# A hybrid stack of three layers: another opening, and side work in fewer steps

## The chip, the cores and the metric

The kernel runs on one core of one Trainium2 chip. The metric is the device time of one execution in microseconds; the lower the better. The kernel before takes 3626.36 us, the median of three runs (3624.73 to 3629.23). A run's time can only be told from another's where they lie apart by more than such spreads.

The engines are called by short names: PE multiplies matrices (PEld loads its weights), DVE and ACT work on vectors element by element, POOL only issues a few transfers here, SP issues the transfers of all weights.

## The reference

Two blocks follow each other on 256 tokens of width 2048, in float32: two hybrid layers (layers 0 and 1 here), then one layer of another kind (layer 2). What matters for this change is the first layer:

```python
mod = jnp.dot(jax.nn.silu(c), w_ada) + b_ada            # c: one vector of 2048, w_ada: 2048 x 6144
shift, scale, gate = jnp.split(mod, 3, axis=-1)
u = rms_norm(x, norm_w) * (1.0 + scale[:, None, :]) + shift[:, None, :]
proj = jnp.dot(u, w_in)                                 # w_in: 2048 x 19064
...
fq, fk  = rms_norm(...)                                 # "fox": 8 heads, full attention with decay
dq, dk  = partial_rope(rms_norm(...), positions)        # "dsa": 8 heads, the keys chosen by an index
iq, ik  = partial_rope(...)                             # 16 index heads of 64: scores, then top 64 of 256
xbc = jax.nn.silu(causal_depthwise_conv(sxbc, conv_w, conv_b))
y = ssd_scan(...)                                       # 4 groups, 2 pieces of 128 tokens
y = y * jax.nn.silu(sz), rms_norm over each group
gates = jax.nn.sigmoid(mg + b_merge)
merged = gates[0] * (y_fox @ w_o_fox) + gates[1] * (y_dsa @ w_o_dsa) + gates[2] * (y_ssd @ w_o_ssd)
x = x + gate[:, None, :] * (merged @ w_out)
```

`u` of the first layer needs `scale` and `shift`, two thirds of a product of one vector with a matrix of 48 MB. They are needed before any projection can start, and their weights are read once only. The same product for layer 1 and the `gate` thirds are worked out later, beside other work.

## The kernel before, in words

**Multiplications.** Every weight matrix is cut into chunks of 1 MB (512 rows by 512 columns, on 128 partitions x 2048). There are 547 of them. To keep float32 precision each factor is split into a high and a low part, and a chunk is multiplied three times (line 1179): high by high, high by low, low by high. A chunk goes through four steps: SP fetches it into a `RAW` buffer (line 1066), ACT copies it rounded into an `HH` buffer (`hi`, line 1434), DVE subtracts and writes the low part into `LL` (`lo`, line 1777; `LL` has the same number as `RAW`), and PE multiplies (`gemm`, in two halves). There are three `HH` buffers and five `RAW`/`LL` buffers; `SP` waits before each fetch until the last reader of its buffer is done, and goes through its fetches in order. What a chunk is multiplied with are `UH`/`UL` (the layer's `u`) or `YH`/`YL`. Chunk numbers below count these multiplications from 0.

**The order.** All engines follow one list of steps written by `work_order` at build time (class `Order`, lines 96 to 345). Between two multiplications stands a `slot`: one step of the lane `evac` (what takes results out of PSUM: `hd` for heads, `conv`, `sz` for the scan's gate, `gate` and `merge`, ...) and one of the lane `side` (everything else: the angles `rope`, the small projections `misc`, index scores `ix`, the selection `ix_top`/`ix_sel`, attention `att`, the scan `ssd`). A lane is a queue of generators; a `yield` ends a step. `yield MID` says that the next part is to be placed between the two halves of the next multiplication (`middle`). Where a multiplication needs the result of a lane's job, `until` takes slots without multiplications until that job is done. `ada_maybe` puts in, at a rate `every`, chunks of `w_ada` of layer 1 and of the `gate` thirds, which DVE multiplies with the vector (`ada`, line 1794, four instructions each) and PE folds (`fold`, line 1207).

**The opening** (`open`, lines 311 to 341) works out `scale` and `shift` of layer 0 in four groups of 4 x 128 columns. In a group there are eight column blocks of 1 MB, four of `scale` and four of `shift`. Five of the eight are summed by DVE from a transposed copy of the weights (`dot_dve`, line 1770: one instruction over 2048 elements with a sum), three by PE (`dot_pe`, line 1196: 16 products with one column each, in two passes, so 32 rows). Then `am` (lines 1864 to 1876) adds the biases, and `u` (lines 1906 to 1929) modulates 512 columns of x on DVE, with ACT's rounded copy (line 1477) and DVE's difference (line 1928) behind it. As soon as `u` has a group, three chunks of projections (two of `iq`, one of `dk`) are multiplied beside the sums of the next group. In the opening there are three more `RAW` buffers, eight in all, used in turn for everything that is fetched. Before the first group x is normalized on ACT (line 1447), turned by PE (line 1217) and copied (line 1438). The angle work `rope`, for tokens and for channels in two parts each (lines 1812 to 1850, on `WW`, tiles `W`), is spread over slots of the first three groups.

**Buffers at the end of the opening.** Fetches 42 and 43 (the last two chunks of the third projection step) go into buffers 0 and 1 again; buffer 0 was last given to chunk 9's weights. Fetch 42 so waits until multiplication 9 is done.

## Time and profile before

| | |
|---|---|
| median of three runs | 3626.36 us |
| the profiled execution | 3630.86 us, its span 3629.1 us |
| PE busy | 3487.7 us (96%), 18836 instructions |
| PE's weight loads | 2994.2 us (83%) |
| DVE busy | 2268.1 us (62%) |
| ACT busy | 1689.1 us (47%) |
| granted TensorE clock, mean | 0.977 |
| DMA | 706.72 MB, mean 195 GB/s |

The profiled execution is one execution of the program; the rows further down are of it. The span runs from the first to the last instruction, and 1.8 us lie around it. Busy time of PE counts pipelined matmuls, so that a matmul of 0.39 us stands beside the next one that starts earlier. In a row of the trace the form `out<-in` names the tiles without their numbers, and what stands in brackets at the end is how long the engine had been idle before, and who released it. A stretch (`A:B`) gives for each engine the busy time and the number of instructions in it, then the clock that was granted to PE (1.00 is 2.4 GHz, 0.50 would be 1.2 GHz throughout), the busy share of the 16 DMA engines and the rate of the transfers.

### The profile page before, as it was taken

Reading aid. Unit: us, or ns where it says so; the run is one execution under the profiler, and the core shown is the slowest. Engines: PE = TensorE matmul, PEld = TensorE weight load, DVE = VectorE, ACT = ScalarE, POOL = GpSimd, SP = SyncE. Lnnn points to the kernel's source line nnn. Section 1 sums busy time; section 2 is a strip of 40 time slices with the busy share of each in tenths; the row PEclk is TensorE's granted clock in tenths of the full one; section 3 lists DMA queues with packets and bytes.
Section 4 is the critical chain, followed back from the end, with each engine's and each line's share of the span. In section 5 each row is a group of like instructions: output and inputs, shape, how many; then the busy total and the mean of one; then the engine's idle time right before and its main releaser. Section 6 shows DMA issues by size and latency. Waiting matters only on the chain. (4 is left out here: it accounts for less than half of the span.)

```text
span 3629.1 us, 45020 instructions
## 1 busy us (share of the span) xinstructions
PE 3487.7 (96%) x18836; PEld 2994.2 (83%) x18836; DVE 2268.1 (62%) x2673; ACT 1689.1 (47%) x2077; POOL 31.1 (1%) x61
## 2 busy tenths in 40 slices
PE   8889999997999999999999999999999999999998
PEld 7779878877887887789888788888888789988887
DVE  5568766765667656677656566765566667554544
ACT  3254654353343334545653553333445775443433
POOL 0000000000000000000000000000000000000000
PEclk8899999998999999999999999999999999999999
DMA  8654445445767655444444357765555443455554
GB/s 346 264 187 149 165 174 209 175 150 203 263 254 272 239 186 197 164 162 151 163 146 145 128 204 258 266 253 195 184 188 185 171 163 142 151 219 186 194 184 154
DMA packets 99531, 706.72 MB, mean 195 GB/s; under 512 B 11696, under 2 KB 11712, under 8 KB 15616
## 3 DMA queue, kind: packets, MB, share of 16 engines
q1 hardware_dynamic: 93888, 675.38, 50.7%
q0 software_dynamic: 4864, 24.95, 2.0%
q8 instruction: 149, 2.44, 0.3%
q10 hardware_dynamic: 576, 3.50, 0.3%
q14 instruction: 54, 0.44, 0.0%
HBM read 697.49 MB, written 6.29 MB: 194 GB/s over the span
## 5 line engine op out<-in xcount | busy, mean ns | idle before, releaser
L1434 ACT ACTIVATE HH<-RAW 128x2048 fp32r<-128x2048 f32 x546 | 1044.8, 1914 | 1204.2 <-PE G L1179 853.8
L1777 DVE TENSOR_TENSOR LL<-RAW,HH 128x2048 fp32r<-128x2048 f32 x546 | 1247.7, 2287 | 349.3 <-ACT HH L1434 347.7
L1179 PE MATMUL G<-HH,UH 128*128 128x512 f32 x2528 | 1019.9, 403 | 38.0 <-DVE LL L1777 35.0
L1179 PE MATMUL G<-LL,UH 128*128 128x512 f32 x2528 | 998.1, 395 | 0.0
L1179 PE MATMUL G<-HH,UL 128*128 128x512 f32 x2528 | 997.9, 395 | 0.0
L1179 PE MATMUL G<-UH,HH 128*128 128x256 f32 x2080 | 607.6, 292 | 17.6 <-DVE XS L2029 9.0
L1179 PEld LDWEIGHTS G<-HH,UH 128*128 128x128 f32 x2528 | 483.2, 191 | 156.3 <-DVE LL L1777 45.3
L1179 PE MATMUL G<-UH,LL 128*128 128x256 f32 x2080 | 592.8, 285 | 0.0
L1179 PE MATMUL G<-UL,HH 128*128 128x256 f32 x2080 | 592.6, 285 | 0.0
L1179 PEld LDWEIGHTS G<-LL,UH 128*128 128x128 f32 x2528 | 482.4, 191 | 103.8
L1179 PEld LDWEIGHTS G<-HH,UL 128*128 128x128 f32 x2528 | 483.4, 191 | 100.9 <-issue 3.6
L1179 PEld LDWEIGHTS G<-UH,HH 128*128 128x128 f32 x2080 | 403.2, 194 | 27.1 <-DVE LL L1777 22.2
L1179 PEld LDWEIGHTS G<-UL,HH 128*128 128x128 f32 x2080 | 403.2, 194 | 2.3 <-issue 1.5
L1179 PEld LDWEIGHTS G<-UH,LL 128*128 128x128 f32 x2080 | 402.6, 194 | 0.0
L1179 PE MATMUL G<-HH,YH 128*128 128x512 f32 x768 | 306.6, 399 | 3.2 <-DVE LL L1777 3.2
L1179 PE MATMUL G<-LL,YH 128*128 128x512 f32 x768 | 304.6, 397 | 0.0
L1179 PE MATMUL G<-HH,YL 128*128 128x512 f32 x768 | 304.3, 396 | 0.0
L1794 DVE SCALAR_TENSOR_TENSOR ACC<-RAW,CT,ACC 128x512 f32<-128x512 f32 x240 | 180.1, 751 | 9.1 <-DMA RAW<-in_w_ada_packed_dram 2.2
L1179 PEld LDWEIGHTS G<-HH,YH 128*128 128x128 f32 x768 | 144.8, 188 | 39.9 <-DVE LL L1777 5.7
L1179 PEld LDWEIGHTS G<-HH,YL 128*128 128x128 f32 x768 | 144.8, 189 | 34.8 <-issue 0.2
L1179 PEld LDWEIGHTS G<-LL,YH 128*128 128x128 f32 x768 | 144.6, 188 | 34.9
L1993 DVE SCALAR_TENSOR_TENSOR S<-G,PAR,S 128x253 f32<-128x253 f32 x144 | 69.2, 480 | 52.2 <-ACT S L1535 48.7
(353 smaller groups left out, 2522.0 us busy)
## 6 DMA issues: line engine op xcount, KB each, us to landing
RAW<-in_w_in_packed_dram SPq DMA_DIRECT2D x402, 1024.0 KB, 4.8
RAW<-in_w_ada_packed_dram SPq DMA_DIRECT2D x76, 1024.0 KB, 4.9
RAW<-in_w_out_packed_dram SPq DMA_DIRECT2D x48, 1024.0 KB, 4.8
RAW<-in_w_o_ssd_packed_dram SPq DMA_DIRECT2D x32, 1024.0 KB, 4.8
RAW<-w_ada_turned_packed_dram SPq DMA_DIRECT2D x20, 1024.0 KB, 12.4
RAW<-in_w_o_fox_packed_dram SPq DMA_DIRECT2D x16, 1024.0 KB, 6.1
RAW<-in_w_o_dsa_packed_dram SPq DMA_DIRECT2D x16, 1024.0 KB, 5.8
RAW<-in_w_proj_a_packed_dram SPq DMA_DIRECT2D x16, 1024.0 KB, 4.8
```

The lines of the kernel that those rows point to most:

```text
L1179: mm = pe.matmul(to, lt, rh, start=first, stop=end, skip_group_check=True)
L1434: a.activation(HH[g % NH][:, :n], RAW[buf(ch["f"])][:, :n], ACT.Copy).then_inc(*hi_done.up(g))
L1777: v.tensor_tensor(LL[buf(f)][:, :n], RAW[buf(f)][:, :n], HH[g % NH][:, :n].bitcast(F32), ALU.subtract).then_inc(*lo_done.up(g))
L1794: v.scalar_tensor_tensor(ACC[:, :], src, CT1[:, kk:kk + 1], ACC[:, :], ALU.mult, ALU.add).then_inc(*ada_acc.up(i, k))
L1993: v.scalar_tensor_tensor(to, of, weight(j), to, ALU.mult, ALU.add).then_inc(*done.up(*key, n))
```

## The change

The change has six parts.

1. *Rings of buffers.* In the opening the column sums get buffers 0 to 3 in turn (`"dots"`), the projection chunks 5, 6, 7 and 4 (`"first"`). Behind the opening, as before, all go through 0 to 4.
2. *Column sums.* In the first group three sums stay on PE, in the others one; DVE takes the rest, 26 in all for 20 before, PE 6 for 12. `am` adds the parts accordingly.
3. *Modulation on ACT.* In layer 0 `u` is worked out on ACT (`Identity` with scale and bias) in place of DVE.
4. *Angle work and x.* The slots of the opening are now in the first group, behind its sums 2 to 7, so that `scaled` and all four `rope` parts stand there; `x_norm` and `x_in` come three sums later.
5. *Side work in fewer steps.* Two `ix_top` to a step; the scan's last step of the first piece (`ssd_y`, c = 0) and the next piece's first step in one slot (`MID`); `misc_sp` 2 and `misc_cs` in one.
6. *Rate of `ada`.* Two slots in five for one in two, from the end of the opening to the convolution.

```diff
--- before.py
+++ after.py
@@ -29,6 +29,12 @@
 NR, NX, NH = 5, 3, 3
+
+
+RINGS = {"dots": (0, 1, 2, 3), "first": (5, 6, 7, 4), "all": tuple(range(NR))}
+
+
+ON_PE = (3, 1, 1, 1)
 HEADS = {"iq": (None, "idx", 4), "dk": ("dsa", "rot", 2), "dq": ("dsa", "rot", 4), "fq": ("fox", None, 4),
@@ -107,7 +113,7 @@
         self.packed = {}
-        self.opening, self.next_buf, self.buf_user = True, 0, {}
+        self.turn_of, self.buf_user = {}, {}
         self.fetches = []
@@ -158,23 +164,24 @@
-    def fetch(self, src, reader):
+    def fetch(self, src, reader, ring="all"):
         name = src[0]
         self.packed[name] = self.packed.get(name, 0) + 1
         f = len(self.fetches)
-        buf = self.next_buf % (NR + NX if self.opening else NR)
-        self.next_buf += 1
+        bufs = RINGS[ring]
+        buf = bufs[self.turn_of.get(ring, 0) % len(bufs)]
+        self.turn_of[ring] = self.turn_of.get(ring, 0) + 1
         self.fetches.append({"src": src, "at": (name, self.packed[name] - 1), "reader": reader, "buf": buf,
                              "before": self.buf_user.get(buf)})
         self.buf_user[buf] = f
         return f
-    def bring(self, ch):
+    def bring(self, ch, ring="all"):
         ch["g"] = len(self.chunks)
         self.chunks.append(ch)
-        ch["f"] = self.fetch(ch["src"], ("gemm_done", ch["g"]))
+        ch["f"] = self.fetch(ch["src"], ("gemm_done", ch["g"]), ring)
         self.put("hi", ch["g"])
@@ -305,7 +312,7 @@
         token = ("dot_" + engine, kind, ct)
-        self.dots[token[1:]] = self.fetch(src, token)
+        self.dots[token[1:]] = self.fetch(src, token, "dots")
         self.put(*token)
@@ -313,29 +320,30 @@
             old = [b["chunks"][gi - 1] if gi else None for b in blocks]
-            dots = [("shift", 1, "pe"), ("scale", 0, "dve"), ("scale", 1, "dve"), ("shift", 2, "pe"), ("scale", 2, "dve"),
-                    ("scale", 3, "dve"), ("shift", 3, "pe"), ("shift", 0, "dve")]
+            on_pe = [("shift", m, "pe") for m in range(4 - ON_PE[gi], 4)]
+            dots = [("scale", m, "dve") for m in range(4)] + [("shift", m, "dve") for m in range(4 - ON_PE[gi])]
+            for i, part in zip((0, 3, 6) if gi == 0 else (2,), on_pe):
+                dots.insert(i, part)
             for i, (kind, m, engine) in enumerate(dots):
                 if i == 7:
                     new = blocks[0]["chunks"][gi]
-                    self.bring(new)
+                    self.bring(new, "first")
                 self.dot(kind, 4 * gi + m, engine)
                 if i in (2, 5) and gi:
                     ch = old[1 + i // 5]
-                    self.bring(ch)
+                    self.bring(ch, "first")
                     self.put("lo", ch["g"])
                 if i in (0, 3) and gi:
                     self.gemm(old[i // 3])
-                    self.slot()
                 if not gi:
                     between(i)
+                    if i > 1:
+                        self.slot()
             enter(gi)
             if gi < 3:
                 self.put("lo", new["g"])
             if gi:
                 self.gemm(old[2])
-                self.slot()
-        self.opening, self.next_buf = False, 0
         self.pend.append(blocks[0]["chunks"][3])
@@ -353,10 +361,10 @@
     def first_x(i):
-        if i == 1:
+        if i == 4:
             put("x_norm", 0)
             put("x_norm", 1)
-        if i == 3:
+        if i == 6:
             for c in range(KT // 2):
@@ -575,7 +583,8 @@
                 put("ix_top", l, qt, i)
-                yield
+                if i % 2:
+                    yield
             put("ix_sel", l, qt)
@@ -595,7 +604,7 @@
                 side_ended("ssd_yd", l, g, c)
-                yield
+                yield None if c else MID
     def misc(l):
@@ -615,7 +624,6 @@
         put("misc_sp", l, 2)
-        yield
         put("misc_cs", l)
@@ -676,7 +684,7 @@
             o.ada["list"] += [(1, b, k) for b in range(8) for k in range(4)]
-            o.ada["every"] = (1, 2)
+            o.ada["every"] = (2, 5)
             misc_b = o.block([one], misc(l), ("U", 0), u_ready, KT)
@@ -1472,6 +1480,17 @@
         def u(l, gi):
+            if l == 0:
+                a.wait_ge(*am.at(0, gi))
+                a.wait_ge(*x_put.at(KT // 2 - 1))
+                for pi in (2 * gi, 2 * gi + 1):
+                    if pi >= 2:
+                        a.wait_ge(*u_lo.at(0, pi - 2))
+                    for j in range(2):
+                        ct = 2 * pi + j
+                        i = a.activation(SS[pi % 2][:, j * S:(j + 1) * S], xsT[:, ct, :], ACT.Identity,
+                                         bias=SH[:, ct:ct + 1], scale=AM[:, ct:ct + 1])
+                    i.then_inc(*u_full.up(0, pi))
             for pi in (2 * gi, 2 * gi + 1):
@@ -1813,6 +1832,7 @@
             if part == 0:
+                v.wait_ge(*ld_cst.at())
                 v.wait_ge(*ld_pos[r].at())
@@ -1863,17 +1883,17 @@
         def am_first(gi):
             c = 4 * gi
+            e = c + 4 - ON_PE[gi]
             pe_part = (BD, BE)[gi % 2]
             v.wait_ge(*ld_mod.at())
             v.wait_ge(*ld_par[0].at())
-            v.wait_ge(*dot_dve.at("shift", c))
+            v.wait_ge(*dot_dve.at("shift", e - 1))
             v.tensor_tensor(AM[:, c:c + 4], DOT[:, 16 + c:20 + c], MOD[:, 16 + c:20 + c], ALU.add).then_inc(*own.up())
-            v.tensor_tensor(SH[:, c:c + 1], DOT[:, c:c + 1], MOD[:, c:c + 1], ALU.add).then_inc(*own.up())
+            v.tensor_tensor(SH[:, c:e], DOT[:, c:e], MOD[:, c:e], ALU.add).then_inc(*own.up())
+            v.wait_ge(*dot_pe.at("shift", c + 3))
+            v.tensor_tensor(SH[:, e:c + 4], pe_part[:, e - c:4], MOD[:, e:c + 4], ALU.add).then_inc(*own.up())
             v.wait_ge(*own.last())
-            v.scalar_tensor_tensor(AM[:, c:c + 4], AM[:, c:c + 4], 1.0, PA[:, c:c + 4], ALU.add, ALU.mult).then_inc(*own.up())
-            v.wait_ge(*dot_pe.at("shift", c + 3))
-            v.wait_ge(*own.last())
-            v.tensor_tensor(SH[:, c + 1:c + 4], pe_part[:, 1:4], MOD[:, c + 1:c + 4], ALU.add).then_inc(*am.up(0, gi))
+            v.scalar_tensor_tensor(AM[:, c:c + 4], AM[:, c:c + 4], 1.0, PA[:, c:c + 4], ALU.add, ALU.mult).then_inc(*am.up(0, gi))
         def am_v(l, gi):
@@ -1905,20 +1925,17 @@
         def u(l, gi):
             for step in range(3):
-                if step < 2:
+                if step < 2 and l:
                     pi = 2 * gi + step
-                    if l:
-                        v.wait_ge(*xn_turned.at(l, pi))
-                    elif pi == 0:
-                        v.wait_ge(*x_put.at(KT // 2 - 1))
+                    v.wait_ge(*xn_turned.at(l, pi))
                     if pi >= 2:
                         v.wait_ge(*u_lo.at(l, pi - 2))
                     else:
                         v.wait_ge(*evac_before("u", l, gi))
-                    v.wait_ge(*am.at(l, 0 if l else gi))
+                    v.wait_ge(*am.at(l, 0))
                     for j in range(2):
                         ct = 2 * pi + j
-                        src = TURN[gi % 2][step][:, j * S:(j + 1) * S] if l else xsT[:, ct, :]
+                        src = TURN[gi % 2][step][:, j * S:(j + 1) * S]
                         i = v.tensor_scalar(SS[step][:, j * S:(j + 1) * S], src, AM[:, ct:ct + 1], SH[:, ct:ct + 1], ALU.mult,
```

What this does to the order is shown at three places, each before and then after. Line numbers of the new kernel are some lines higher: L1789 is the column sum (L1770 before), L1796 the split `lo` (L1777 before).

The first place is DVE in the first group, from the first column sum to the first split of a chunk. `RAW,DOT<-RAW,CB` are column sums, `WW` the angles, `RST` the norm of x, `AM` and `SH` the entry. Before:

```order
L1770 SCALAR_TENSOR_TENSOR RAW,DOT<-RAW,CB 128x2048
L1854 RECIPROCAL RST<-RST 128x1 x2
L1770 SCALAR_TENSOR_TENSOR RAW,DOT<-RAW,CB 128x2048 x4
L1870 TENSOR_TENSOR AM<-DOT,MOD 128x4
L1871 TENSOR_TENSOR SH<-DOT,MOD 128x1
L1873 SCALAR_TENSOR_TENSOR AM<-AM,PAR 128x4
L1876 TENSOR_TENSOR SH<-BD,MOD 128x3
L1922 TENSOR_SCALAR S<-XS,AM,SH 128x256 x4
L1928 TENSOR_TENSOR UL<-S,UH 128x512 x2
L1777 TENSOR_TENSOR LL<-RAW,HH 128x2048
```

and now, with the angle instructions that follow each other cut to the first ones (`...`):

```order
L1789 SCALAR_TENSOR_TENSOR RAW,DOT<-RAW,CB 128x2048 x2
L1829 TENSOR_SCALAR PAR<-PAR 128x1
L1848 CAST WW<-WW 128x2
...
L1789 SCALAR_TENSOR_TENSOR RAW,DOT<-RAW,CB 128x2048
L1874 RECIPROCAL RST<-RST 128x1 x2
L1854 TENSOR_SCALAR WW<-WW 128x96
...
L1789 SCALAR_TENSOR_TENSOR RAW,DOT<-RAW,CB 128x2048
L1843 CAST WW<-WW 128x256
...
L1789 SCALAR_TENSOR_TENSOR RAW,DOT<-RAW,CB 128x2048
L1891 TENSOR_TENSOR AM<-DOT,MOD 128x4
...
L1945 TENSOR_TENSOR UL<-S,UH 128x512 x2
L1796 TENSOR_TENSOR LL<-RAW,HH 128x2048
```

All angle work moved in front of the first `AM`, the norm's reciprocals moved behind the third sum, and the four modulations (`S<-XS,AM,SH`) are gone from DVE.

The second place is DVE at the scan's gate in layer 0: `SM`, `XS` and `S` rows belong to `sz`, `MOD` to a fold, `ACC` to `ada`, `LL` to the chunks. PE's transpose for `XS<-BE,PAR` stands between the row above it and that row. Before, at the last group of the gate:

```order
L1777 TENSOR_TENSOR LL<-RAW,HH 128x2048
L2022 RECIPROCAL SM<-SM 128x1
L2024 TENSOR_SCALAR XS<-XS,SM 128x512
L2029 TENSOR_TENSOR XS<-BE,PAR 128x512
L2014 SCALAR_TENSOR_TENSOR S<-S,G 128x512
L2017 SCALAR_TENSOR_TENSOR XS<-S,XS 128x512
L2022 RECIPROCAL SM<-SM 128x1
L2024 TENSOR_SCALAR XS<-XS,SM 128x512
L2029 TENSOR_TENSOR XS<-BE,PAR 128x512
L1806 TENSOR_TENSOR MOD<-BE,MOD 128x4
```

and now at the same last group:

```order
L1796 TENSOR_TENSOR LL<-RAW,HH 128x2048
L2046 TENSOR_TENSOR XS<-BE,PAR 128x512
L2031 SCALAR_TENSOR_TENSOR S<-S,G 128x512
L2034 SCALAR_TENSOR_TENSOR XS<-S,XS 128x512
L1796 TENSOR_TENSOR LL<-RAW,HH 128x2048
L2039 RECIPROCAL SM<-SM 128x1
L2041 TENSOR_SCALAR XS<-XS,SM 128x512
L1796 TENSOR_TENSOR LL<-RAW,HH 128x2048
L2046 TENSOR_TENSOR XS<-BE,PAR 128x512
L1825 TENSOR_TENSOR MOD<-BE,MOD 128x4
```

and at the second group, where a fold now stands:

```order
L1796 TENSOR_TENSOR LL<-RAW,HH 128x2048
L2046 TENSOR_TENSOR XS<-BE,PAR 128x512
L2031 SCALAR_TENSOR_TENSOR S<-S,G 128x512
L2034 SCALAR_TENSOR_TENSOR XS<-S,XS 128x512
L2039 RECIPROCAL SM<-SM 128x1
L2041 TENSOR_SCALAR XS<-XS,SM 128x512
L2046 TENSOR_TENSOR XS<-BE,PAR 128x512
L1825 TENSOR_TENSOR MOD<-BE,MOD 128x4
L1810 TENSOR_SCALAR ACC<-RAW,CT 128x512
L1813 SCALAR_TENSOR_TENSOR ACC<-RAW,CT,ACC 128x512 x3
```

Before, the last two steps of the gate and the fold stood between two multiplications, with no `LL` row between them. Now an `LL` row stands between each pair there, and the pile is at the second group instead.

The third place is DVE at the small projections of layer 0. `WW<-WW 40x256` are `misc_sp` 2, `FF`, `T` and `CS` are `misc_cs`, `RR` and `S` a head (`hd`), and PE's `misc_turn` waits for the end of `misc_cs`. Before:

```order
L2126 TENSOR_TENSOR WW<-WW 40x256
L2128 SCALAR_TENSOR_TENSOR WW<-WW 40x256
L1777 TENSOR_TENSOR LL<-RAW,HH 128x2048
L1939 RECIPROCAL SM<-SM 128x4
L1946 SCALAR_TENSOR_TENSOR S<-G,SM,ROWS 128x128 x4
L1962 TENSOR_TENSOR RR<-S,RT 128x128
L1963 TENSOR_TENSOR RR<-S,RT 128x4x16
L1964 TENSOR_TENSOR RR<-S,RT 128x4x16
L1966 TENSOR_TENSOR S<-RR 128x4x32
L2142 SCALAR_TENSOR_TENSOR FF<-CST,WW 8x256
L2145 TENSOR_SCALAR FF<-FF 8x256
```

and now:

```order
L1983 TENSOR_TENSOR S<-RR 128x4x32
L2134 TENSOR_SCALAR WW<-WW 40x256
L2136 SCALAR_TENSOR_TENSOR WW<-WW 40x256
L2137 SCALAR_TENSOR_TENSOR WW<-WW 40x256
L2139 RECIPROCAL WW<-WW 40x256
L2141 TENSOR_TENSOR WW<-WW 40x256
L2143 TENSOR_TENSOR WW<-WW 40x256
L2145 SCALAR_TENSOR_TENSOR WW<-WW 40x256
L2159 SCALAR_TENSOR_TENSOR FF<-CST,WW 8x256
L2162 TENSOR_SCALAR FF<-FF 8x256
```

Before, a chunk's split and a head stood between the two parts. Now they are one piece behind the head.

## Rows read from the trace of the kernel before

**Rows 1.** Stretches: PE, PEld, DVE, ACT, POOL busy; clock, DMA share, GB/s.

```profile
38.90:73.60 34.70, 34.16 (x172) 30.00 (x172) 23.43 (x34) 9.65 (x8) 0.00 (x0) 0.74 0.85 346
73.60:106.50 32.90, 32.90 (x169) 28.39 (x168) 28.80 (x49) 8.02 (x8) 0.00 (x0) 0.81 0.84 335
106.50:141.70 35.20, 35.20 (x175) 30.27 (x175) 21.39 (x23) 7.01 (x5) 0.00 (x0) 0.80 0.71 291
...
20.00:40.00 20.00, 15.76 (x89) 14.41 (x89) 9.67 (x13) 13.61 (x16) 0.00 (x0) 1.00 1.02 423
343.00:375.00 32.00, 30.17 (x246) 29.21 (x245) 28.33 (x55) 14.07 (x20) 0.00 (x0) 1.00 0.42 151
800.00:900.00 100.00, 75.22 (x491) 69.83 (x490) 56.01 (x60) 39.70 (x35) 2.13 (x4) 0.87 0.51 186
```

**Rows 2.** DVE in order of time: start, duration, line, operation, tiles; the opening.

```profile
38.94 0.16 DVE L1870 TENSOR_TENSOR AM<-DOT,MOD 128x4 f32<-128x4 f32 x1
...
41.36 1.38 DVE L1922 TENSOR_SCALAR S<-XS,AM,SH 128x256 f32<-128x256 f32 x4
...
73.64 0.16 DVE L1870 TENSOR_TENSOR AM<-DOT,MOD 128x4 f32<-128x4 f32 x1
...
141.70 0.17 DVE L1870 TENSOR_TENSOR AM<-DOT,MOD 128x4 f32<-128x4 f32 x1
```

**Rows 3.** PE in order of time, opening and early layer 0.

```profile
54.90 3.63 PE L1196 MATMUL BE<-CT,RAW 128*128 128x1 f32 x32
...
59.28 0.63 PE L1179 MATMUL G<-HH,UH 128*128 128x512 f32 x1
...
62.58 0.39 PE L1179 MATMUL G<-LL,UH 128*128 128x512 f32 x1
...
62.81 0.39 PE L1179 MATMUL G<-HH,UH 128*128 128x512 f32 x1
...
163.90 0.79 PE L1179 MATMUL G<-HH,UH 128*128 128x512 f32 x1 [9.02 <-DVE LL L1777]
...
208.12 0.80 PE L1179 MATMUL G<-HH,UH 128*128 128x512 f32 x1 [4.40 <-DVE LL L1777]
...
258.50 0.44 PE L1268 MATMUL BA<-CST,T 128*128 128x128 f32 x2 [2.55 <-ACT T L1653]
```

**Rows 4.** SP in order of time, behind the opening.

```profile
154.91 1.87 SPq L1066 DMA_DIRECT2D RAW<-in_w_in_packed_dram  x4
```

**Rows 5.** The W tiles alone, 0 to 200 us, columns as in rows 1.

```profile
0.00:200.00 200.00, 0.00 (x0) 0.00 (x0) 10.19 (x36) 1.40 (x4) 1.06 (x2) 0.85 0.74 294
```

**Rows 6.** Line 1770, the column sums on DVE: shortest/median/longest ns, starts.

```profile
L1770 DVE SCALAR_TENSOR_TENSOR RAW<-RAW,CB x20: 2280/2288/2293, 16.4 to 139.3; 128x2048 f32<-128x2048 f32 x20
```

**Rows 7.** ACT in order of time: entry, and a convolution step.

```profile
42.13 1.28 ACT L1477 ACTIVATE UH<-S 128x512 fp32r<-128x512 f32 x2 [2.14 <-DVE S L1922]
...
275.51 0.56 ACT L1535 ACTIVATE S<-G,PAR 128x256 f32<-128x256 f32 x1 [4.63 <-PE G L1179]
```

**Rows 8.** DVE in order of time: small projections and selection, layer 0.

```profile
242.50 0.29 DVE L2117 TENSOR_SCALAR WW<-WW 40x256 f32<-40x256 f32 x1
...
246.33 0.42 DVE L2128 SCALAR_TENSOR_TENSOR WW<-WW 40x256 f32<-40x256 f32 x1
...
362.31 0.42 DVE L2242 MAX8 SM<-WW 128x8 f32<-128x256 f32 x1
...
364.27 2.29 DVE L1777 TENSOR_TENSOR LL<-RAW,HH 128x2048 fp32r<-128x2048 f32 x1
```

**Rows 9.** PE's waits, 800 to 900 us: total us, times, longest.

```profile
PE BE L1286 <- DVE XS L2024: 12.2, 3, 7.3
PE G L1179 <- DVE XS L2029: 5.3, 1, 5.3
...
PE BE L1207 <- DVE XS L2029: 0.9, 1, 0.9
```

**Rows 10.** The page, costliest groups: the `ada` products on DVE.

```profile
L1794 DVE SCALAR_TENSOR_TENSOR ACC<-RAW,CT,ACC 128x512 f32<-128x512 f32 x240 | 180.1, 751 | 9.1 <-DMA RAW<-in_w_ada_packed_dram 2.2
```

## The prediction, made before the changed kernel was run

> **What bounds the kernel now.** I read the page first, then the stretches, then the opening on each engine in order of time, then PE's waits. On the page PE is busy for 3487.7 of 3629.1 us, so only what PE waits for, what it does needlessly, and its clock are worth anything: 141 us of idle time. The stretches show two places where most of that lies: the first 200 us, and 800 to 900 us, where PE is busy for 75 us at a granted clock of 0.87 [rows 1]. The rest of the change must be read against a PE that is full.
>
> In the opening the reader should see the cadence of the four groups. Each ends with the first instruction of `am` on DVE: four such rows, the first at 38.9, the second at 73.6, the last at 141.7 us [rows 2], on average 34.3 us apart; three of the stretches are cut there. In these three stretches PE is busy all the time (34.2 of 34.7, then 32.9 and 35.2 in full) at a granted clock of 0.74 to 0.81, DVE for 21 to 29 us, DMA at a share of 0.71 to 0.85 [rows 1]. PE sets the cadence. A group on PE is three column sums of 3.63 us [rows 3] and three chunk multiplications, which so take (34.3 - 10.9) / 3 = 7.8 us each. They would be shorter at full clock: behind a column sum the matmuls take 0.63 us (at 59.28), and some 3 us later 0.39 (at 62.58) [rows 3], the 1.2 and the 2.4 GHz level. At the higher one they start 0.23 us apart (62.58 and 62.81), 24 of them in 5.6 us.
>
> At the end of the opening PE waits 9.0 us at 163.90 [rows 3]: four weight fetches in a row could start only at 154.91 [rows 4], because the next buffer was still read by the multiplication before.
>
> **The opening after the change.** Loads of a group, each against the cadence of 34.3:
> - PE: one column sum in place of three, 3 x 7.8 + 3.6 = 27.0 us at the clock of before, less if the stretches at 1.2 GHz go with the sums.
> - DVE: 73.6 us busy in the three groups [rows 1], of which some 9.8 us are angle work (10.2 us on the W tiles up to 200 us [rows 5], 36 instructions, all in this opening) that now stands in the first group. That leaves 21.3 a group; minus 1.4 for the modulation that ACT takes over, plus two more sums of 2.2 (2.29 us each, 20 of them now [rows 6], overlapping by 0.08) = 24.3, plus a wait for ACT of about 2.3 inside each entry = 26.6 us.
> - ACT: the modulation. On DVE four instructions took 1.38 us [rows 2]. ACT with scale and bias per partition took 0.56 us for one of this size out of PSUM [rows 7]; out of SBUF no row shows it. Bounds: 1.4 us for four (as DVE) to 2.3 (4 x 0.56); I take 2.1, nearest the only ACT row. ACT is idle enough to hide it, but the entry is a chain, DVE's split waits behind it: +0.7 us a group.
> The Trainium skill (ScalarE: Activation LUTs, Rules for kernel authors) advises VectorE and not ScalarE for multiply and add, and its section What ACT_TABLE_LOAD costs gives 186 ns + 0.833 ns an element + about 93 ns for each per-partition operand. An estimate from that is 0.585 us each, about 2.1 us for four; the trace agrees with its 0.56. By the rule alone the move would cost 0.7 us in each of four entries.
> - DMA: 11 transfers of 1 MB. From 20 to 40 us the DMA share is 1.02 at 423 GB/s [rows 1], 2.48 us a transfer: 27.3 us.
> So three resources meet at 27, and that is the floor. I take 29.5 for the second and third interval: the modulation ring has four buffers, SP issues in order, and one buffer in each turn is held by PE's sum, which stands behind a multiplication that itself waits for the entry. Two or three fetches stand behind it, and DMA idles for 2 to 3 us.
>
> The first group gets later. All the angle work comes into it: 11.3 us of DVE time with its gaps. It fits partly into the time that DVE now waits there for transfers, but the norm's reciprocals, the transposes and ACT's copies of x queue behind the sines. Walking down the new order with the durations above: four sums, four angle parts, `am` at about 45 us instead of 38.9 (41 with PE's part, behind which the modulation starts at 41.36 [rows 2]), and the first multiplication at about 54 us. The ring then refills only from there, so the first interval is 33 us. `am` of the last group: 45 + 33 + 2 x 29.5 = 137 us against 141.7.
>
> The end of the opening gains more. The buffers of the last fetches are freed by sums that are done long before, so the 9.0 us wait goes. From `am` to the second multiplication behind it: 0.5 + 2.1 + 1.3 (ACT's two copies [rows 7]) + 0.7 + 2.2 for the split (2.29 us at 364.27 [rows 8]) + 7.3 for one multiplication = 14 us, before 163.9 - 141.7 = 22.2. It starts at 151 instead of 163.9: **-13 us**. Bounds: -27 (`am` first at 41, as now, then 27.3 three times: 123 + 14 = 137) and -2 (45 + 3 x 34.3 + 14 = 162).
>
> **The side work after the change.** It changes nothing in what is computed, only how many steps share one multiplication.
> - *Gating in layer 0* (`sz`). PE now waits 12.2 us in three waits of its transposes for VectorE, 5.3 for a gate chunk and 0.9 for the fold [rows 9]: 18.4 us. The last six `sz` steps and a fold stand between two multiplications. Now fox attention ends four chunks sooner, and each of the last steps has a multiplication beside it. What is late next: a pile of the same kind behind chunk 87, with half a multiplication (2.8 us) to cover it: 7.3 - 2.8 + 0.9 = 5.4 us, and one transpose of 4.1. Loss 9.5 (with the longest wait of 7.3 [rows 9] and a guess of 4.1, a third of the 12.2) for 18.4, and about 4 of the 10 us that the clock of 0.87 takes from the 75 busy ones [rows 1]: **-13**, bounds -18 and 0 (a wait that proves to be the weights' DMA stays).
> - *`misc_sp` 2 and `misc_cs` in one step.* In layer 0 they now run between a `hd` and PE's `misc_turn`. The part moved in is 242.50 to 246.75, 4.25 us [rows 8]; now PE waits 2.55 us at that place [rows 3]. With one half multiplication less it becomes some 7 to 8: **+5**, bounds 0 and +6. In layer 1 the step stands alone, nothing.
> - *`ix_top` two to a slot.* From 343 to 375 us DVE is busy 28.3 of 32 us [rows 1], so it already is nearly the bound in a slot of 6.5 us; one pair of 8-wide maxima at 256 takes 362.31 to 364.27, 1.96 us [rows 8]. Four slots get 1.4 to 2 us more than they have room for; lookahead hides one or two us of about 7: **+5**, bounds 0 and +8.
> - *`gate` 0, an `ada` chunk and `gate` 1 piled up* behind chunks 106, 118 and 130, where PE now waits for nothing: 0.7 + 3.0 + 2.2 + 0.7 us of DVE against one multiplication of 5.6: **+3**, bounds 0 and +5.
> - *Fewer `ada` chunks early* (2 in 5 for 1 in 2): one chunk of four, some 3 us (4 x 0.75 [rows 10]), leaves the path in front of the 4.4 us wait at 208.12 [rows 3]: **-3**, bounds -4 and 0.
> Sum: -13 - 13 + 5 + 5 + 3 - 3 = **-16 us**. Against the profiled execution's 3630.9 us (span 3629.1, 1.8 us around it) that is 3615; the median of the three runs, 3626.4, is 4.5 us lower, so I forecast **3610 us**.
>
> **Rivals.**
> - *B, the loads decide* (cadence 27.3, the first group hides its angle work). For it: DVE waits for transfers in the first group, and PE's clock may rise with six sums fewer. Against: SP's queue is in order, and DVE, DMA and PE would have to fit with no slack at all. -27 in place of -13: 3596.
> - *C, the ring of four keeps the old cadence.* Before, up to eight transfers were under way; now four for sums. If each PE sum blocks the queue as long as PE takes for a multiplication at the low clock, the intervals stay near 34: -2 in place of -13, side work as above: 3621; with the gating worth nothing too, 3634. Taken together about 3626.
> - *D, slower: VectorE becomes the bound where side work was packed.* One mechanism: from chunk 30 to 57 each slot in layer 0 gets the convolution and a bigger step (two maxima; then attention up to chunk 47; then two steps of the scan with a fold, against a multiplication of some 6 us). It decides if DVE needs over 7 us a slot in more than ten slots: 10 to 15 slots x 2 us = +25 in place of +5, opening as forecast: 3630 to 3640, say 3635. For it: 28.3 of 32 us busy [rows 1]. Against: the attention slots cost PE an extra us too, and the same work is missing later.
>
> **Chances.** Forecast 0.48, its own range 3600 to 3620; B 0.20; C 0.17; D 0.15. What a measurement here can tell from no change is about 0.2%, 7 us. Faster takes B and nearly all of the forecast, 0.65; same takes C and the forecast's upper edge, 0.20; slower takes D, 0.15. The range runs from B's 3592 to 3633, where half of D is left out.
>
> **What the profile will show.** `am` at 45, 78, 107, 137 us; if it is 41, 68, 96, 123 then B, if the intervals are 34 then C. DMA share near 0.9 in these intervals and SP waiting for PE's sum. Column sums on PE: 6 behind 3.6 us each, granted clock above 0.85 from 50 to 140. No 9 us wait in front of the second multiplication behind the last `am`. Between the last attention step and the fg chunks in layer 0 PE waits of 9 us in place of 18, the largest at a transpose. A wait of 7 to 8 us at `misc_turn` in layer 0. DVE over 95% busy for four slots around 320 to 345 us. The forecast is wrong if the start of the second multiplication behind the opening moves by under 5 us, or if PE's idle time between 250 and 600 us grows by over 15.

## The result and the profile after

The changed kernel takes 3646.23 us (median of nine runs, 3640.01 to 3648.63) for 3629.23 before on the same chips: 1.0044 of it, 95% interval 1.0033 to 1.0055. It is 0.44% slower (17 us), where 16 us less were forecast. Its profiled span is 3640.9 us, 11.8 more than before.

The first view is the table of stretches. Its first three lines are the groups of the opening and answer to the first three of [rows 1], the last to the last there:

```profile
44.37:78.58 34.21, 24.80 (x108) 20.00 (x106) 24.03 (x23) 11.73 (x13) 0.00 (x0) 0.80 0.73 286
78.58:108.81 30.23, 23.51 (x104) 19.59 (x104) 24.09 (x24) 8.85 (x9) 0.00 (x0) 0.83 0.91 365
108.81:139.52 30.71, 24.36 (x106) 19.57 (x104) 24.20 (x23) 8.87 (x9) 0.00 (x0) 0.83 0.95 383
...
800.00:900.00 100.00, 86.15 (x538) 78.74 (x537) 67.81 (x70) 39.84 (x34) 1.60 (x3) 0.91 0.56 208
```

PE is no longer full in the opening (25 of 34 us), and in the second and third stretch the transfers nearly are (0.91 and 0.95). From 800 to 900 us PE is busy for 86 us, 75 before. DVE in order of time answers to [rows 2]; the two entries between these start at 78.58 and 108.81:

```profile
44.37 0.16 DVE L1891 TENSOR_TENSOR AM<-DOT,MOD 128x4 f32<-128x4 f32 x1
...
139.52 0.16 DVE L1891 TENSOR_TENSOR AM<-DOT,MOD 128x4 f32<-128x4 f32 x1
```

and ACT in order of time shows the modulation where [rows 7] had only its stand-in:

```profile
47.37 2.06 ACT L1491 ACTIVATE S<-XS,SH,AM 128x256 f32<-128x256 f32 x4
```

PE in order of time answers to [rows 3]: the first multiplication behind the last `am`, the first row of the second (the 25th from there; no wait stands in front of it), and `misc_turn`:

```profile
146.24 0.79 PE L1187 MATMUL G<-HH,UH 128*128 128x512 f32 x1 [6.46 <-DVE LL L1796]
...
153.92 0.39 PE L1187 MATMUL G<-HH,UH 128*128 128x512 f32 x1
...
239.90 0.69 PE L1276 MATMUL BA<-CST,T 128*128 128x128 f32 x2 [8.01 <-ACT T L1672]
```

PE's waits from 750 to 1160 us answer to [rows 9] and reach further, since a wait that was not there before stands on top (two small ones, 3.1 us together, are left out):

```profile
PE G L1187 <- ACT WW L1597: 10.7, 4, 2.7
PE BE L1294 <- DVE XS L2041: 8.8, 4, 4.7
PE G L1187 <- DVE LL L1796: 7.0, 5, 2.5
PE BE L1215 <- DVE YL L2086: 5.1, 1, 5.1
...
```

**A ledger by chunk.** Both kernels have the same chunks, so the start of ACT's copy `HH` of chunk g, minus the same start before, says how far ahead (-) a kernel is. Worked out from the timelines, one profiled execution of each kernel, in us (`new opening alone` is `o_only` below, `with the new rate` `o_rate`, `with MID only` `o_mid`):

| chunk | new opening alone | with the new rate | with MID only | changed kernel |
|---|---|---|---|---|
| 10 | -16.1 | -17.1 | -14.3 | -16.5 |
| 20 | -9.7 | -21.3 | -10.4 | -21.2 |
| 40 | -9.7 | -12.2 | -8.8 | -4.0 |
| 60 | -9.7 | -22.5 | -9.5 | 0.5 |
| 85 | -8.9 | -22.8 | 7.0 | 14.9 |
| 98 | -2.9 | -36.6 | 0.4 | -18.9 |
| 150 | -1.7 | -13.3 | -0.7 | 3.7 |
| 250 | -3.3 | -13.8 | 0.7 | -0.3 |
| 260 | -3.3 | -13.8 | 12.4 | 13.3 |
| 300 | -3.2 | -13.8 | 11.6 | 12.6 |
| end | -4.2 | -12.3 | 10.8 | 11.8 |

The last column tells where the time went: 21 us won by chunk 20 (half of it, the rate's, is gone again by chunk 30, in `o_rate` too), lost again by chunk 60, won once more at the gating (chunk 98), lost in the merge branches (98 to 150) and in layer 1 (250 to 260).

Such a column can be read to some 5 us only. `a_phase1` and `a_fix` below have the same order of work as the changed kernel up to the merge branches. Yet at chunk 85 they stand at 20.8 and 18.8 us, where the changed kernel stands at 14.9. In chunks 80 to 85 the same 224 instructions took PE 46.5 us in the changed kernel and 49.7 in each of the other two, at a granted clock of 1.00 and 0.93, with no wait.

### The profile page after: what moved, and what is told of

It reads as the page before. It is cut to its first block and busy times, and to the rows that moved or that the text cites. A ratio compares the mean times of both kernels' runs of the same rounds, so it can differ in the third digit from the quotient of the medians.

```text
span 3640.9 us, 44638 instructions
## 1 busy us (share of the span) xinstructions
PE 3465.1 (95%) x18644; PEld 2968.7 (82%) x18644; DVE 2276.1 (63%) x2669; ACT 1703.2 (47%) x2099; POOL 31.1 (1%) x61
## 5 line engine op out<-in xcount | busy, mean ns | idle before, releaser
L1796 DVE TENSOR_TENSOR LL<-RAW,HH 128x2048 fp32r<-128x2048 f32 x546 | 1248.2, 2287 | 365.5 <-ACT HH L1442 364.2
L1187 PE MATMUL G<-UH,HH 128*128 128x256 f32 x2080 | 607.6, 292 | 18.9 <-DVE LL L1796 12.5
L1187 PEld LDWEIGHTS G<-UH,HH 128*128 128x128 f32 x2080 | 403.2, 194 | 27.7 <-DVE LL L1796 22.8
```

Source lines behind the costliest of these rows:

```text
L1187: mm = pe.matmul(to, lt, rh, start=first, stop=end, skip_group_check=True)
L1796: v.tensor_tensor(LL[buf(f)][:, :n], RAW[buf(f)][:, :n], HH[g % NH][:, :n].bitcast(F32), ALU.subtract).then_inc(*lo_done.up(g))
```

## Experiments

Times are medians; the kernel before took 3629.7, 3629.8, 3631.3 and 3631.4 us in the four groups of runs. "The kernel of 3591 us" in the expectations is `best` below.

**One part alone.** `o_only` is the changed kernel with four lines put back:

```diff
-                if i % 2:
-                    yield
+                yield                               # ix_top
-                yield None if c else MID
+                yield                               # scan
+        yield                                       # between misc_sp 2 and misc_cs
-            o.ada["every"] = (2, 5)
+            o.ada["every"] = (1, 2)
```

> The new opening (rings, column sums, modulation on ACT, angle work) with all side work as before. Theory 1 (the opening gave what its stretch shows, and side work took it back): the copy of chunk 20 stands 18 to 21 us earlier than before, and the gap stays to the end; about 3611 us, 0.5% faster than before. Theory 2 (time gained in the opening is given back by whatever stands behind it, as the clock or the weights' transfers): the gap shrinks behind chunk 30; 3622 to 3632 us.

Measured 3626.36 us, ratio 0.9991 (0.9982 to 1.0000): a miss for theory 1, whose 18 to 21 us by chunk 20 were the opening's and the rate's together. The time is that of theory 2, but the gap does not shrink behind chunk 30: the opening's own 9.7 us stand in the ledger (8.9 at chunk 85); then, up to chunk 90, 6 go, with the same order of work as before and no new wait. A stretch of chunks 86 to 88 shows most of it, first in the kernel before:

```profile
726.38:747.14 20.76, 20.76 (x104) 15.63 (x104) 13.62 (x26) 9.70 (x24) 0.00 (x0) 1.00 0.23 87
```

and with the new opening alone:

```profile
717.43:742.95 25.52, 25.52 (x105) 19.37 (x104) 14.29 (x26) 9.70 (x25) 0.00 (x0) 0.80 0.19 72
```

The work is the same and the granted clock differs. What lowered it is open. These are two single executions, and the clock can differ so between executions of one order, as above; but the medians agree that of the 9.7 us some 3 are left.

`o_rate` keeps the `(2, 5)`, `o_mid` the `MID`:

> The new opening and, of the side work's changes, only the rate of two slots in five. Theory 1 (the rate alone sets against which steps of the gate and of the scan's gating a fold falls): the pile of six sz steps and a fold behind chunk 94 is gone, the piles behind chunks 106, 118, 130 and 142 are there, each with a PE wait of 2.7 us for ACT; -16 there, +18 here, -2 early: within 5 us of the kernel with the new opening alone, 3611 us. Theory 2 (what moved the piles is that fox attention ended four chunks earlier, as the prediction said): both piles as before, since attention is not shortened here; 3608 us from the early gain alone.

> The new opening and, of the side work's changes, only the scan's joined steps (MID). Theory 1 (the joined step costs in both layers): layer 1 is 12 to 16 us longer between chunks 250 and 275, with PE waiting for DVE in its decay products, and layer 0 by some 5; 3625 to 3632 us. Theory 2 (the loss of layer 1 belongs to attention that begins earlier behind shorter selection): layer 1 within 3 us of before from chunk 245 to 300; 3611 us.

`o_rate`: 3612.29 us, 0.9957 (0.9945 to 0.9970). Attention is not shortened in it, yet the pile at chunk 94 goes and the four piles at the gates come: theory 1. Of the 12.2 us in three waits of [rows 9] this is left in it from 750 to 1160 us:

```profile
PE BE L1294 <- DVE XS L2041: 3.1, 3, 1.3
```

Its gain is 14 us over `o_only`, more than either expected. A third pile, behind chunk 54, goes too (PE waits 1.0 us there for 4.0): 14 us between chunks 54 and 60, of which half are lost again by chunk 70. `o_mid`: 3638.30 us, 1.0025 (1.0015 to 1.0036), 12 us slower than `o_only`, most of it between chunks 250 and 260: theory 1 (its 3625 to 3632 stood on an `o_only` of 3611).

**The four waits of 2.67 us.** In the merge branches one slot of the changed kernel holds `gate` 0, an `ada` chunk, `gate` 1 and a `merge`. On ACT, in order of time:

```profile
907.36 1.91 ACT L1442 ACTIVATE HH<-RAW 128x2048 fp32r<-128x2048 f32 x1 [3.17 <-PE G L1187]
909.18 0.61 ACT L1597 ACTIVATE WW<-WW 128x512 f32<-128x512 f32 x1
```

and on PE:

```profile
909.93 0.47 PE L1187 MATMUL G<-HH,UH 128*128 128x512 f32 x1 [2.67 <-ACT WW L1597]
```

The gate's `tanh` stands in ACT's queue behind a chunk's copy; the copy waits for the end of PE's multiplication, and PE's next one waits for the `tanh`: 1.91 + 0.61 us and the signals. DVE's work is not in it: the product of the merge waits for the same `tanh` (2.70 us). `a_phase1` moves the `ada` counter on by one slot ahead of the branches, so that folds fall elsewhere:

```diff
         o.ada["every"] = (1, 3)
+        o.ada["count"] += 1
```

> The changed kernel, and the ada counter is moved on by one slot ahead of the merge branches, so that no fold falls against a gate. Theory 1 (the four piles cost 4 x 5 us): none of the waits of 2.7 us for ACT is left between chunks 100 and 152, 18 us less than the changed kernel, 3628 us. Theory 2 (the multiplications there are slower for another cause, as the clock): 3 us or less; 3643 us.

3632.98 us, ratio 1.0008 (0.9999 to 1.0017), 13 less than the changed kernel: nearer to theory 1. The four waits are gone, and at chunk 150 it is 19 us ahead of the changed kernel; but the line runs in layer 1 too, and puts two folds against gates there: PE waits 5.3 us in two waits for the same row. `a_fix` and `best` (on `o_rate`) have `+= 1 if l == 0 else -1`:

> The changed kernel with the counter one slot further in layer 0's merge branches and one back in layer 1's, so that no fold falls against a gate in either layer. Theory 1 (six waits of 2.67 us told the two kernels apart; none is left): 3628 us, 18 less than the changed kernel. What it then stands above 3591 us (37 us) is the price of the three joined steps together. Theory 2: the shift is worth no more than in the kernel with the shift in both layers: 3633 us.

> The new opening with the rate of two in five, all other side work as before, and the ada counter one slot further in layer 0's merge branches (and one back in layer 1's, where the shift alone had put two folds against gates). Theory 1 (each fold against a gate costs about 5 us): the four PE waits of 2.67 us for ACT are gone and none comes in layer 1; 18 us less than with the rate alone, about 3594 us. Theory 2 (the shift only moves the loss to another place, as it did in layer 1): 3608 to 3615 us.

3628.82 us, 0.9993 (0.9984 to 1.0003), and 3591.22 us, 0.9892 (0.9879 to 0.9906). The piles cost 17 us in the changed kernel and 21 in `o_rate`: theory 1 both times. In `best`, which runs up to 45 us ahead there, PE's waits from 750 to 1120 us are these:

```profile
PE G L1188 <- DVE LL L1797: 6.3, 5, 2.4
PE BE L1295 <- DVE XS L2042: 3.0, 3, 1.3
PE G L1188 <- DVE XS L2047: 2.2, 1, 2.2
```

The waits for ACT and the one of 5.1 us for `YL` are gone with the shift, in `a_fix` as well. The 8.8 us for `XS` are still there in `a_fix`; they belong to the joined steps.

**The joined steps, one by one**, added to `best` (the lines of the change), and the scan's taken from `a_fix`:

> The kernel of 3591 us (new opening, rate of two in five, no fold against a gate), with two ix_top to a step added. Theory 1 (the prediction's: DVE has 1.4 to 2 us too much in four slots): 5 us slower, 3596 us, layer 0 alone. Theory 2 (all but the first slot is hidden): within 2 us.

> The kernel of 3591 us, with misc_sp 2 and misc_cs in one step added. Theory 1: PE's wait at misc_turn in layer 0 grows from 2.5 to 8 us and nothing gives it back, 5.5 us slower, with a dip of the granted clock behind it perhaps 7: 3597 us. Theory 2 (the step saved is won later): within 2 us.

> The changed kernel without folds against gates (3629 us), and with the scan's joined steps undone. Theory 1 (the joined steps cost 10 us in layer 0, for the gating's pile behind chunk 87 then has attention in it, and 14 in layer 1): 3605 us, and this is the 3591 us kernel plus 10 and 4 for the two other joins. Theory 2 (the joins of selection and small projections cost more together than alone): 3612 us or more.

`b_ix` 3601.13 (0.9920, 0.9908 to 0.9933), `b_misc` 3595.43 (0.9906, 0.9893 to 0.9920), `a_nomid` 3598.08 us (0.9911, 0.9896 to 0.9926). So `ix_top` costs 10 alone (twice theory 1 of `b_ix`), the small projections 4 (near theory 1 of `b_misc`, and within the spread of the runs), both together 7 (3598.1 - 3591.2), and `MID` 31 us (3628.8 - 3598.1): `a_nomid` is 7 us below its theory 1, and `MID` costs more than there and than alone. That the two others don't add up is not shown: at chunk 250 `b_ix` stands 7.0 us behind `best`, `b_misc` 2.0 and `a_nomid` 8.9. From chunk 280 to 290 `a_nomid` then wins 4.7 of them, with the same 416 instructions on PE: 85.5 us at a granted clock of 1.00, where the kernel before and `best` have 90.2 us at 0.94.

The stretch from chunk 250 to 260, without `MID` (`a_nomid`):

```profile
1738.00:1807.00 69.00, 68.25 (x341) 56.23 (x340) 39.17 (x40) 41.06 (x84) 0.00 (x0) 1.00 0.42 150
```

and with it (`a_fix`):

```profile
1751.50:1833.50 82.00, 77.95 (x369) 63.41 (x368) 43.27 (x47) 48.89 (x94) 0.00 (x0) 0.94 0.36 128
```

No engine but PE is near its bound. `a_fix` does more in its stretch (369 instructions on PE for 341), and waits more. What is late is one chain: with `ssd` and the first decay step under one multiplication, PE reaches the scan's product before DVE has its operand. PE in order of time, in `a_fix`:

```profile
1809.08 3.68 PE L1385 MATMUL BD<-XD,WW 128*128 128x64 f32 x16 [2.38 <-DVE WW L2295]
```

and the same product, the third of eight in layer 1, in `a_nomid`, where none of them waits:

```profile
1796.57 1.89 PE L1385 MATMUL BD<-XD,WW 128*128 128x64 f32 x16
```

From chunk 250 to 290 PE waits 6.7 us in `a_fix` and 1.1 in `a_nomid`. The clock comes on top: PE's busy time, times one minus the granted clock, summed over stretches of ten chunks, is 11 us for 0. Of these 11 only 6 are the joined step's, for the kernel before and `best` lose 5 there as well (chunks 280 to 290 above). A ledger of the two kernels gives 13 us for layer 0 (up to chunk 250) and 17 for layer 1, of which 4.7 are that clock. Between `o_mid` and `o_only`, where `MID` stands alone, it gives 4 us for layer 0 and 11 for layer 1. Layer 1 thus agrees (12.7 and 11); why layer 0 costs 13 in company and 4 alone, no run here takes apart.

**The opening's parts**, each undone on `best`: modulation on DVE by the old `u` (`b_udve`), and

```diff
-ON_PE = (3, 1, 1, 1)                               # b_pe3
+ON_PE = (3, 3, 3, 3)
-            for i, part in zip((0, 3, 6) if gi == 0 else (2,), on_pe):
+            for i, part in zip((0, 3, 6), on_pe):
-RINGS = {"dots": (0, 1, 2, 3), "first": (5, 6, 7, 4), "all": tuple(range(NR))}     # b_ring8
+RINGS = {"open": tuple(range(NR + NX)), "all": tuple(range(NR))}
+        ring = ring if ring == "all" else "open"
-                    if i > 1:                      # b_rope; slots behind the multiplications
-                        self.slot()                # of groups 2 to 4 again, x_norm at i == 1,
                                                    # x_in at i == 3
```

`n_rate` is the kernel before with only the rate and the counter's shift.

> As the kernel of that last row, with the modulation of the first layer back on DVE. Theory 1 (four entries, each with four operations of 0.52 us on ACT for 0.35 on DVE): 3 us faster than with ACT, since the entry is a chain. Theory 2 (DVE's relief is worth more): 3 to 6 us slower, since DVE's sums stand behind it.

> As that kernel, with three column sums of every group on PE. Theory 1 (PE with three sums set the cadence of 34 us): am of the last group moves from 139.5 to 146 us or later, 7 to 12 us slower. Theory 2 (the rings set it): within 3 us.

> As that kernel, with all fetches of the opening through one ring of eight buffers. Theory 1 (what the rings gave is the wait of 9.0 us at the second multiplication behind the opening, and what they cost is about 3 us of DMA time in each group): the cadence falls from 30.5 to 28.5 us and the wait of 9 is back; 3 us slower in all. Theory 2 (the ring of four costs nothing in the groups): 9 us slower.

> The kernel of 3591 us with the angle work back in the second and third group and x normalized earlier in the first. Theory 1 (the angle work delays the first am by 5 us and the later groups are bound by the loads, so they hide it): am first at 39 us, the later ones 3 to 5 us earlier, 3587 us. Theory 2 (DVE bounds the later groups): 3 to 5 us slower, 3595 us.

> The kernel before, its old opening untouched, with only the rate of two in five and the counter shifted so that no fold falls against a gate. Theory 1 (the new opening is worth the 10 us that its stretch shows): 10 us slower than the kernel that has both, 3601 us. Theory 2 (the new opening is worth 3 us, as the medians with the old rate say): 3594 us.

| kernel | us | ratio to before, interval | last `am`, us |
|---|---|---|---|
| `best` | 3591.22 | 0.9892, 0.9879 to 0.9906 | 140.4 |
| `b_udve` | 3585.59 | 0.9874, 0.9861 to 0.9888 | 138.3 |
| `b_pe3` | 3588.44 | 0.9891, 0.9876 to 0.9906 | 139.8 |
| `b_ring8` | 3603.25 | 0.9929, 0.9916 to 0.9942 | 141.9 |
| `b_rope` | 3590.46 | 0.9886, 0.9871 to 0.9900 | 137.6 |
| `n_rate` | 3599.95 | 0.9911, 0.9896 to 0.9926 | 143.9 |

The whole opening is worth 8.7 us (`n_rate` less `best`: theory 1; the ledger has 8.6 at chunk 30), and the rings carry it: without them 12 us are lost, 11.7 of them by chunk 12. This is nearer to theory 2: the cadence does not fall (`am` at 44.4, 79.2, 110.9, 141.9 us), and the old wait is back in front of the second multiplication:

```profile
166.41 0.79 PE L1189 MATMUL G<-HH,UH 128*128 128x512 f32 x1 [9.28 <-DVE LL L1798]
```

Modulation on ACT costs 5.6 us by the medians of four runs each, and the two intervals overlap; theory 1 said 3, and 3.3 us is how far `b_udve` is ahead at chunk 12. The place of the column sums (theory 2 of `b_pe3`) and of the angle work (between its theories) make no difference that can be told; the last `am` moves by 0.6 and 2.8 us.

**A faster version.** `fin1` is `b_udve` with the `ada` rate behind the convolution at one slot in three and the counter placed by hand; `fin3` adds three column sums a group on PE.

```diff
             o.ada["every"] = (2, 5)
+            o.ada["count"] += 2
...
-        o.ada["every"] = (2, 5) if l == 0 else 0
+        o.ada["every"] = (1, 3) if l == 0 else 0
+        o.ada["count"] += 2
...
         o.ada["every"] = (1, 3)
-        o.ada["count"] += 1 if l == 0 else -1
+        o.ada["count"] += 2 if l == 0 else 0
```

> The kernel of 3591 us, with the modulation on DVE (3586 us) and the ada chunks thinned to one slot in three behind the convolution, the counter placed so that folds fall beside neither gates nor the last sz steps. Theory 1 (piles in front of a multiplication are what costs): 3575 to 3583 us. Theory 2 (pieces of attention in the pile behind chunk 87 already covered it): 3583 to 3590 us.

> The kernel of 3583 us (modulation on DVE, fewer ada chunks) with three column sums of every group on PE. Theory 1 (PE and the loads each take about 30 us a group, so that it makes no difference): within 3 us of 3583. Theory 2 (a PE that is busy keeps the higher clock behind the opening): 3 to 6 us faster.

3583.33 us, 0.9870 (0.9856 to 0.9883), and 3583.83 us, 0.9868 (0.9851 to 0.9886): 1.3% faster than before. Theory 2 for `fin1`: over `b_udve` it is 2 us, not clear of the spread. Theory 1 for `fin3`.

## Why the prediction was wrong

The medians make a chain of five links, set beside the terms of the forecast:

| term | forecast | measured | from |
|---|---|---|---|
| opening | -13 | -8.7 | `best` - `n_rate` |
| gating -13, `ada` -3 | -16 | -31.4 | `n_rate` - before |
| piles at the gates | +3 | +17.4 | changed - `a_fix` |
| `ix_top` +5, `misc` +5 | +10 | +6.9 | `a_nomid` - `best` |
| joined scan step | none | +30.7 | `a_fix` - `a_nomid` |
| sum | -16 | +14.9 | |

(The changed kernel's own comparison with before gives 17. By the ratios to before, which take out the differences between the groups of runs, the links are -7, -32, +18.5, +7 and +30, with an uncertainty of 5 to 7 us each by their intervals; the first and the fourth are hardly clear of it.)

**The step that failed** is the first sentence of the part on the side work: "It changes nothing in what is computed, only how many steps share one multiplication." Under it the joined scan step got no price in the sum. It is 31 us, in both layers, while the sum has no term for layer 1 at all; behind it in layer 1 is PE's wait for DVE in front of the scan's product, and a lower granted clock; what makes up the 13 us of layer 0 stays open. Without this term the chain sums to -15.8, the forecast; that is luck, since of the other terms one was half and another a sixth of what was measured. Rival D named it in passing, but from chunk 30 to 57 and with DVE's load as the cause. The second step that failed is the piles at the gates, 17.4 us for 3.

**Right sum, wrong cause.** Gating, `ada` rate and gate piles were put at -13 together and came to -14, by luck. But the prediction let attention's earlier end undo the pile of chunk 94. `o_rate` has that pile gone with attention as long as before: a fold occupies the lane `evac`, and the rate of `ada` decides beside which step it falls. Its gain was twice the size (of the 31 us, 19 stand between chunks 94 and 98 in the ledger of `n_rate`), its price at the gates six times: 17.4 for 3. That price was worked out from DVE's durations, while PE waited for ACT's queue.

**The opening** went as told: `am` at 44.4, 78.6, 108.8, 139.5 us (45, 78, 107, 137), modulation 2.06 us for four (2.1; one takes 0.585 us, as estimated), no wait of 9 us, the second multiplication at about 154 (151), 10 us earlier than before. The 3 us missing are the three intervals, each about 1 us longer than forecast; from the last `am` to the second multiplication it took the 14 us of the sum. In the medians the opening is worth 8.7 us beside the new rate, and only 3.3 with the old one (`o_only`). (The 16 us at chunk 10 in the ledger are a copy's; before, the copies of chunks 10 to 12 followed within 5 us once their fetches could start.) Rivals B and C are out: the intervals were 34.2, 30.2 and 30.7. (The lower end of the range, 3592, is put down to B, whose sum is 3596.)

**The Trainium skill's rule** (ScalarE: Activation LUTs, Rules for kernel authors) is to use VectorE and not ScalarE for multiply and add. The trace agrees: 2.06 us for 1.38, the 0.7 us that the prediction put beside the rule for each of four entries. Undoing the move won 3.3 us by chunk 12, near the 2.7 of the four, and 5.6 in the medians; the rest is within their spread.

**`misc_turn`** waits 8.0 us as forecast (7 to 8), and costs 4.2 for 5. **`ix_top`** costs 10 alone for 5, past its bound of 8 (7.0 in the ledger at chunk 250). Rival D's 3635 was the nearest to the time, but its mechanism is seen only in this small part: from chunk 30 to 57 PE waits for DVE's splits 9.2 us in the changed kernel and 3.1 in `o_rate`, where D wanted 20 and more.

**The signs that were named.** The two that were to tell that the forecast is wrong did not: the second multiplication moved by 10 us, and PE's idle time from 250 to 600 us grew by 4.7 (from 18.5 to 23.2). They looked neither at the merge branches nor at layer 1. PE's waits between chunks 85 and 98 fell from 21 to 12 us (18 to 9 were forecast). The clock from 44 to 140 us was 0.82, not above 0.85, and DVE was busy for 22.5 of the 25 us from 320 to 345, not over 95%.

## What to carry to other kernels

A list of steps that is filled at a rate has a phase: before a rate is changed, look at what each inserted step falls beside, in every layer, and move the counter by one to price it. A joined step must be priced by the chain that ends at the waiting engine's next instruction, not by busy time; and a removed slot counts in every layer that runs it. A part has to be priced in the company in which it will run: the scan's joined step cost 12 us alone and 31 here. And before a ledger of single executions is read for a few microseconds, two executions of the same order should be laid side by side.

## What the hardware showed beyond that

A short wait of PE can cost more than itself. The sixteen products of the scan took 1.89 us without a wait, about 2.0 behind waits of up to 1.33 us, and 3.68 behind 2.38 us: the higher and the lower level of the clock. In between either was seen. At one place, behind the same wait of the same order of work, first in the changed kernel and then in `a_fix`:

```profile
642.35 2.00 PE L1384 MATMUL BD<-XD,WW 128*128 128x64 f32 x16 [1.90 <-DVE WW L2294]
```

```profile
641.51 3.62 PE L1385 MATMUL BD<-XD,WW 128*128 128x64 f32 x16 [1.90 <-DVE WW L2295]
```

(`a_phase1`: 3.68 behind 1.90.) So the clock behind a wait is not set by the order of work alone, and one execution does not tell its price. The clock can also be 0.80 with PE busy throughout and the same work at 1.00 in another kernel (chunks 86 to 88 above), or 0.93 and 1.00 in executions of the same order (chunks 80 to 85); no run here says why.
